# Softmax probabilities normalised on VectorE behind the reciprocal, in place of GpSimd, in a two-layer hybrid attention backbone

## What is computed

```python
s = jnp.einsum('bqhgd,bkhd->bhgqk', qi, k) * scale      # (A, D; B adds a sink logit, C a bias)
p = jax.nn.softmax(s, axis=-1)
o = jnp.einsum('bhgqk,bkhd->bqhgd', p.astype(v.dtype), v)
...
up = jnp.einsum('btnw,nwd->btnd', o, w_branch)
g = jax.nn.sigmoid(gate_pre.reshape(up.shape))
y = jnp.sum(g * up, axis=2) @ w_out
```

## Time and profile before

| | |
|---|---|
| median of 3 runs | 1847.69 us (1842.06 to 1847.75) |
| profiled execution | 1853.63 us |
| its span, first to last instruction | 1851.8 us |
| mean granted PE clock | 0.978 |
| PE busy | 1742.4 us (94%) |
| DVE busy | 1185.2 us (64%) |
| ACT busy | 864.6 us (47%) |
| POOL busy | 585.8 us (32%) |
| first layer's attention stage | about 99 to 715 us |
| second layer's attention stage | about 1205 to 1600 us |

### The profile page before, as it was taken

The page is one execution under the profiler, slowest core; times in us unless marked ns, Lnnn a source line. Parts: engine busy times, 40 slices in busy tenths (PEclk is TensorE's granted clock), DMA queues, the critical chain, the costliest instruction groups (busy, mean ns, idle before and its releaser), DMA issues. The chain is left out here.

```text
span 1851.8 us, 29906 instructions
## 1 busy us (share of the span) xinstructions
PE 1742.4 (94%) x9859; PEld 1474.1 (80%) x9859; DVE 1185.2 (64%) x2379; ACT 864.6 (47%) x1860; POOL 585.8 (32%) x555
## 2 busy tenths in 40 slices
PE   7999999999899899899999999888999998999998
PEld 3777877777778778788888887777888777879997
DVE  5357588787677766567777663456564456756655
ACT  4566554444344443542222222556555454555543
POOL 0345443454444452111111000224335654321100
PEclk9999999999999999999999999889999999999999
DMA  8222333434334235244556654234343323446665
GB/s 294 63 67 66 75 93 91 104 112 119 105 86 103 81 69 165 86 130 146 149 157 209 217 186 70 70 83 96 88 119 103 98 75 81 126 137 182 184 201 158
DMA packets 344706, 224.10 MB, mean 121 GB/s; under 512 B 58038, under 2 KB 322540, under 8 KB 344556
## 3 DMA queue, kind: packets, MB, share of 16 engines
q1 hardware_dynamic: 335148, 215.88, 41.6%
q10 hardware_dynamic: 9408, 6.32, 1.3%
HBM read 221.06 MB, written 1.07 MB: 120 GB/s over the span
## 5 line engine op out<-in xcount | busy, mean ns | idle before, releaser
L2073 PE MATMUL bank<-Uhi,w_ring 128*128 128x512 f32 (+1 forms) x1536 | 549.5, 358 | 22.9 <-ACT H L1736 5.4
L2075 PE MATMUL bank<-Uhi,w_ring 128*128 128x512 f32 (+1 forms) x1536 | 533.5, 347 | 0.0
L2074 PE MATMUL bank<-Ulo,w_ring 128*128 128x512 f32 (+1 forms) x1536 | 533.5, 347 | 0.0
L1596 ACT ACTIVATE w_ring<-load_ring 128x512 fp32r<-128x512 f32 (+3 forms) x632 | 369.2, 607 | 151.5 <-PE bank L2075 111.7
L1817 DVE TENSOR_TENSOR w_ring<-load_ring,w_ring 128x512 fp32r<-128x512 f32 (+1 forms) x424 | 317.9, 766 | 171.8 <-ACT w_ring L1596 145.2
L2073 PEld LDWEIGHTS bank<-Uhi,w_ring 128*128 128x128 f32 x1536 | 296.0, 193 | 65.0 <-ACT H L1736 8.0
L2075 PEld LDWEIGHTS bank<-Uhi,w_ring 128*128 128x128 f32 x1536 | 295.8, 193 | 36.6
L1551 POOL TENSOR_TENSOR w_ring<-load_ring,w_ring 128x512 fp32r<-128x512 f32 (+3 forms) x208 | 247.7, 1197 | 239.2 <-ACT w_ring L1596 121.7
L2074 PEld LDWEIGHTS bank<-Ulo,w_ring 128*128 128x128 f32 x1536 | 296.2, 193 | 30.2
L1539 POOL TENSOR_TENSOR Y<-Y,small 128x512 f32<-128x512 f32 x160 | 172.1, 1076 | 299.2 <-DVE small L2017 284.8
L2022 DVE TENSOR_TENSOR Z<-bank,Z 128x512 fp32r<-128x512 f32 x160 | 109.9, 687 | 121.7 <-ACT Z L1721 120.3
(11 more groups left out here) (147 smaller groups left out, 2497.1 us busy)
## 6 DMA issues: line engine op xcount, KB each, us to landing
load_ring<-in_w_in SPq DMA_DIRECT2D x192, 256.0 KB, 2.9
load_ring<-in_w_ffn_in SPq DMA_DIRECT2D x160, 256.0 KB, 3.1
mod_ring<-in_w_mod SPq DMA_DIRECT2D x96, 256.0 KB, 3.3
load_ring<-in_w_ffn_out SPq DMA_DIRECT2D x88, 256.0 KB, 3.2
mod_place<-in_w_mod SPq DMA_DIRECT2D x64, 256.0 KB, 2.8
load_ring<-in_w_branch SPq DMA_DIRECT2D x48, 256.0 KB, 2.9
mod_w<-in_w_mod SPq DMA_DIRECT2D x16, 512.0 KB, 9.9
load_ring<-in_w_in SPq DMA_DIRECT2D x64, 128.0 KB, 2.5
```

Of the source, the lines that this page charges most:

```text
L1596: act.activation(w_ring[:, plan.slot['w', key], 0, 0:sz], load_ring[:, plan.slot['load', key], 0:sz], ACT.Copy).then_inc(sem['w_hi'], 1)
L2073: pe.matmul(dst, lhs[0], rhs[0], start=start, stop=False)
L2074: pe.matmul(dst, lhs[0], rhs[1], start=False, stop=False)
L2075: return pe.matmul(dst, lhs[1], rhs[0], start=False, stop=stop)
```

## The change

The multiplication of the probabilities by the reciprocal of their row leaves POOL's program. It stands in DVE's program directly behind the reciprocal, in the same step `den`, as one `tensor_scalar` for each range of `subs`: one of 128x512 for an `x` item, two of 128x256 for a `c` item. DVE waits there for its own reciprocal and for the place in `Pn`. The order of the steps, the buffers and the signals stay as they were.

```diff
@@ -1529,17 +1529,6 @@
-                elif kind == 'den':
-
-                    pool.wait_ge(sem['rec_ready'], count['rec_ready', key])
-                    for name, k_ in plan.freed['Pn', key]:
-                        pool.wait_ge(sem[name], count[name, k_])
-                    m = len(subs(key))
-                    w = NTOK // m
-                    pool.tensor_tensor(prob('Pn', key).rearrange("p (m k) -> p m k", m=m),
-                                       prob('P', key).rearrange("p (m k) -> p m k", m=m),
-                                       small[:, plan.slot['small', key], 10:10 + m].unsqueeze(2).to_broadcast([P, m, w]),
-                                       ALU.mult).then_inc(sem['prob_ready'], 1)
@@ -2015,6 +2004,12 @@
                     dve.reciprocal(sm[:, 10:10 + m], sm[:, at:at + m]).then_inc(sem['rec_ready'], 1)
+                    dve.wait_ge(sem['rec_ready'], count['rec_ready', key])
+                    for name, k_ in plan.freed['Pn', key]:
+                        dve.wait_ge(sem[name], count[name, k_])
+                    for i, (a, b) in enumerate(subs(key)):
+                        ins = dve.tensor_scalar(prob('Pn', key)[:, a:b], prob('P', key)[:, a:b], sm[:, 10 + i:11 + i], None, ALU.mult)
+                    ins.then_inc(sem['prob_ready'], 1)
```

## The result

The changed kernel takes 1883.47 us (median of 4 runs, 1880.8 to 1888.6) against 1847.48 us before: ratio 1.0205, 95% interval 1.0176 to 1.0234, 36 us slower. The forecast was slower by 14 us, 1861.7, with a range up to 1882. The direction was right and the size was not; the result is 1.5 us beyond the range. The profiled executions differ by 29 us (1853.63 and 1882.7). Lines move in the changed kernel: L2017 is now the remainder of the transposed probabilities (L2022 before), L2333 the value product (L2338), L1702 the exponential (L1713), L1989 the negative maximum (L2000), L1827 the modulation's weighing (L1838), L1540 POOL's low weights (L1551), and L2011 is the new product.

A forecast was written before the change was run, and what follows sets the result against it. PE was taken to bound the kernel; 11 us at places already waiting for DVE plus 2.5 us at joining places, 14 us, on the median 1847.69 gave 1861.7 us. Range 1844 to 1882, the forecast's own 1853 to 1878.

The forecast's parts named there:

- What bounds the kernel: PE, busy 94% of the span; 31 PE waits, 33.7 us, end with DVE's work or the exponential, POOL costs 3 us.
- What goes: POOL loses 160 multiplications, 172.1 us; PE gets back at most 2.6 + 0.6 us.
- What comes: On DVE, 0.58 us per `x` item and 0.80 us per `c` item, 99.8 us in all, 0.62 us an item.
- Relief: DVE operations lengthened by POOL's work in the first attention stage get shorter: about 13 us, bounds 0 and 37.5 us.
- What reaches PE: DVE's delays behind the new instruction reach PE at 31 waiting places and some just short of waiting: 14 us.
- the lower end: Delays don't pile up: 0.35 us more at each of 31 places, 11 us, plus 2.5 us for joining places.
- the upper end: Delays pile up until DVE's next idle time: 0.82 us at each of 31 places, 25 us.
- 57%: Share of L2022's cases, 91 of 160, where DVE did not idle in front of it, so the delay goes on.
- The dense-stretches rival: DVE sets the pace in its densest 300 us, capped at 86% busy: 18 us on top of 14, 1880 us; chance 0.17.
- The faster rival: POOL's release and ended collisions win in the softmax chain of `c` items: 12.6 us faster, 1835 us; chance 0.14.
- Hidden: DVE's idle time in both attention stages absorbs the added work: no change, 1847.7 us within 5.5 us; chance 0.25.
- The signs: PE's waits for remainder and exponential grow to 13 to 15 us, both attention stages grow, L1838 falls near 560 ns.

The follow-up runs named there:

- reduce_beside_pool: Kernel before, product still on GpSimd, plus one 128x512 maximum on VectorE behind its reciprocal whose result nobody reads; 1886.68 us, ratio 1.0191.
- short_low_before: Kernel before, with POOL's low weights writing only 16 columns once a ring slot has been filled; 1816.83 us, ratio 0.9822.
- The pairs with freed VectorE time: Changed kernel and kernel before, both with POOL's low weights, or both with first-layer modulation weighing, cut to 16 columns; gaps 1.0082 and 1.0106.
- slack_places: Changed kernel with the product on VectorE only in first-layer branch A and the whole second layer, elsewhere on GpSimd; 1856.35 us, ratio 1.0043.
- second_layer: Changed kernel with the product on VectorE in the second layer alone (64 items), on GpSimd in the first; 1851.99 us, ratio 1.0015.

## Why the prediction was wrong in size

**What bounds the kernel** held: PE's waits behind DVE took most of the loss (the remainder alone 19.3 of 29 us), and POOL's relief gave nothing that shows (the reduce_beside_pool run has none of it and is as slow).

**What goes** held: POOL's busy time fell to 420 us (414 forecast), PE's wait for its weights stayed 2.6 us.

**What comes** was too small at one term. The sum had 0.62 us an item, 99.8 us in all, and set the collisions of the 192 operations, priced at 13 us beside it, off against as much relief; they are some 35 us. The estimate by the rule of the Trainium skill (SBUF — State Buffer, "Who interferes with whom"), 38 us, set beside it and not used, was close. The 67 ns came from L1836, which has only 32 instances there, in other places of the queue. The 0.10 us for DVE's wait for its own reciprocal was too much: the product begins 0.03 to 0.04 us behind it (243.57 + 0.16 to 243.76 above). The new product takes 118.4 / 160 = 0.74 us, and with that wait 0.78 us an item.

**Relief** of 13 us was credited against this and hardly came: L1838 is at 603 ns (599), and only the two-column L2000 fell, to 351 (624), 24 x 0.273 = 6.6 us. short_low_before, where L1838 fell to 482 ns with the multiplication still on POOL, shows that it waited for POOL's low weights.

**What reaches PE** is the step that failed. I took the lower end, in which delays do not pile up because each stall of PE gives DVE its length back; the upper end was 0.62 x 0.57 / 0.43 per place. The item's size is the smaller part of the miss: with the measured 0.78 us the lower end, with its places that join, is some 18 us, 4 of the 22 that were missing. The upper end is then 0.78 x 0.57 / 0.43 = 1.03 us over 31 places, 32 us, against 36 measured. But one formula with one share, 57%, for all stretches gets near by an average only: by branch the cost is 0.5 us for 64 items where DVE was 60% busy and 9.8 us for 24 where it was 82%. The pairs with freed VectorE time (14 and 21 us in place of 36) show that the missing term is DVE's free time in the stretch. That a stall gives DVE back its length was not measured by itself; if it does, it did not keep the delays from piling up in B, C and D.

**The dense-stretches rival** (+32 us, given 0.17) named the right mechanism and nearly the size. Its price was wrong in detail: DVE was not capped at 86%; B is at 123.28 / 140.3 = 88% after. And it is a matter of degree: C and D, at 74 and 76%, paid as well.

**The faster rival** rested on collisions ending; the two-column operation did become shorter, but PE waited for the exponential as long as before, and ACT waited for the negative maximum 150.9 us where it had waited 115.6. **Hidden** was true for the second layer (2.8 us) and less so for branch A: slack_places less second_layer leaves 4.4 us for its 24 items, 0.18 us each.

**The signs** I had named: ACT's wait for the negative maximum grew as forecast; PE's wait for the remainder grew to 28.3 us and not 13 to 15, the exponential's did not grow, both attention stages were to grow and the first did (616 to about 645 us), the second hardly (395 to 397), and L1838 did not fall. The feed-forward stages kept their length. The forecast of which chain would pay was half right.

## What to carry to other kernels

Price work that is put into an in-order queue by stretch, against the free time which that engine has there, and not over the whole span: here the products of 88 moved items cost 8 us and those of the other 72, by subtraction, about 29. To test such a price without the change, add an idle operation of the same length at the same place; one run of it gave the whole loss. And an operation that another engine's instructions can hold up is better costed with that engine's busy share times half of one of its instructions (38 us here, 35 measured) than from a few instances of a neighbour.

## What the runs showed of the hardware that was not expected

A VectorE product between SBUF places that began while GpSimd ran a 1.30 us operation ended 0.28 us after that operation (1.14 us instead of 0.49), while the form with an accumulator takes 746 ns for 512 columns, and 83 ns more to read the accumulator, and at most 750 beside the same GpSimd work. And leaving out all but 16 columns of GpSimd's low weights made the kernel 32 us faster, although PE waits for them 2.6 us: what they cost VectorE, 26 us in L1838 alone, shows as longer operations there and not as a wait for them.
